# Strassen products for 16 of 22 row tiles of the FFN down projection, set between the gate/up tiles

## The reference

```python
D_FF = -(-8 * D_MODEL // (3 * 256)) * 256          # 2816
def _swiglu(x, w_gu, w_down):
    gate, up = jnp.split(x @ w_gu, 2, axis=-1)
    return (jax.nn.silu(gate) * up) @ w_down
...
        h = _layernorm(ALPHA * h + mix, ln_mix_g[i], ln_mix_b[i])
        h = _layernorm(ALPHA * h + _swiglu(h, ffn_w_gu[i], ffn_w_down[i]), ln_ffn_g[i], ln_ffn_b[i])
```

## Time and profile before

| | |
|---|---|
| median of three executions | 2300.27 us |
| the profiled execution | 2299.87 us |
| its span, first to last instruction | 2298.1 us |
| mean granted clock of TensorE | 0.996 of full |
| busy share PE / DVE / ACT / POOL | 98% / 31% / 31% / 45% |
| read from HBM | 211.02 MB, 93 GB/s over the span |

### The profile page before, as it was taken

One profiled execution on the slowest core, in us unless ns is written; L12 is line 12 of the kernel. 1 busy time (PEld: TensorE's weight loads), 2 busy tenths in 40 slices (PEclk: granted clock), 3 DMA queues, 4 the chain that ended last, 5 costly groups with the idle time before them and its releaser, 6 DMA issues.

```text
span 2298.1 us, 24743 instructions
## 1 busy us (share of the span) xinstructions
PE 2259.6 (98%) x10303; PEld 1826.6 (79%) x10303; DVE 702.9 (31%) x1405; ACT 708.3 (31%) x1009; POOL 1025.3 (45%) x350
## 2 busy tenths in 40 slices
PE   8999999999999999999999999999999999999998
PEld 6667888888777778888888888888887667888887
DVE  7535000003467450010048420000159625000004
ACT  2453221221344332213222232222235572221220
POOL 3224554554332345545445655445433334554453
PEclk9999999999999999999999999999999999999999
DMA  4122323222212232222222332322212213222221
GB/s 173 60 89 98 122 93 109 92 74 92 92 69 79 74 110 92 94 108 83 101 93 98 108 110 96 106 92 83 101 64 102 77 43 147 92 92 94 105 77 55
DMA packets 33535, 214.72 MB, mean 93 GB/s; under 512 B 3720, under 2 KB 4872, under 8 KB 10000
## 3 DMA queue, kind: packets, MB, share of 16 engines
q1 hardware_dynamic: 32256, 211.03, 26.2%
q10 hardware_dynamic: 1168, 2.11, 0.3%
HBM read 211.02 MB, written 2.11 MB: 93 GB/s over the span
## 4 chain that ended last, share of the span: by engine, by line
PE 89%; DVE 8%; ACT 2%; issue 1%; POOL 1%; DMA 0%; SPq 0%; DVEq 0%; ACTq 0%
PE bank L1005 17%; PE bank L1007 16%; PE bank L1006 16%; PE bank L1055 9%; PE bank L1057 9%; PE bank L1056 9%; DVE bank L2138 3%; PE bank L1200 2%; PE bank L1195 2%; PE bank L1196 2%; PE bank L1499 1%; PE bank L1240 1%; PE bank L1473 1%; PE bank L1094 1%; PE bank L1116 1%
## 5 line engine op out<-in xcount | busy, mean ns | idle before, releaser
L848 POOL TENSOR_TENSOR wlo<-raw,whi 128x2048 fp32r<-128x2048 f32 (+5 forms) x184 | 843.3, 4586 | 657.0 <-ACT whi L479 647.0
L1005 PE MATMUL bank<-XH,whi 128*128 128x512 f32 x1720 | 678.7, 395 | 6.2 <-POOL wlo L904 6.2
L1007 PE MATMUL bank<-XH,wlo 128*128 128x512 f32 x1720 | 671.2, 390 | 0.0
L1006 PE MATMUL bank<-XL,whi 128*128 128x512 f32 x1720 | 670.9, 390 | 0.0
L479 ACT CAST whi<-raw 128x2048 fp32r<-128x2048 f32 (+5 forms) x184 | 349.4, 1901 | 378.1 <-PE bank L1055 304.3
L1005 PEld LDWEIGHTS bank<-XH,whi 128*128 128x128 f32 x1720 | 323.8, 188 | 86.2 <-issue 14.0
L1007 PEld LDWEIGHTS bank<-XH,wlo 128*128 128x128 f32 x1720 | 323.7, 188 | 68.4
L1006 PEld LDWEIGHTS bank<-XL,whi 128*128 128x128 f32 x1720 | 324.0, 188 | 65.0
L1811 DVE TENSOR_TENSOR hf<-sil,bank 128x512 f32<-128x512 f32 x80 | 55.0, 688 | 814.4 <-PE bank L1007 814.4
L1055 PE MATMUL bank<-whi,HH 128*128 128x512 f32 x704 | 274.4, 390 | 0.0
L1057 PE MATMUL bank<-wlo,HH 128*128 128x512 f32 x704 | 274.0, 389 | 0.0
(11 more groups left out here) (280 smaller groups left out, 2172.2 us busy)
## 6 DMA issues: line engine op xcount, KB each, us to landing
raw<-w_ffn_gu SPq DMA_DIRECT2D x88, 1024.0 KB, 4.9
raw<-w_ffn_dn SPq DMA_DIRECT2D x40, 1024.0 KB, 4.8
GB<-gb SPq DMA_DIRECT2D x8, 1024.0 KB, 6.9
raw<-w_diff_in SPq DMA_DIRECT2D x6, 1280.0 KB, 6.5
raw<-w_ev_in SPq DMA_DIRECT2D x6, 1024.0 KB, 5.0
raw<-w_od_in SPq DMA_DIRECT2D x4, 1536.0 KB, 6.5
raw<-w_mla_pair SPq DMA_DIRECT2D x4, 1088.0 KB, 5.5
raw<-w_mla_o SPq DMA_DIRECT2D x4, 1024.0 KB, 5.9
```

What stands on the lines that cost most here:

```text
L848: pool.tensor_tensor(wlo[:, off:off + size], raw[:, off:off + size], whi[:, off:off + size].bitcast(F32), ALU.subtract).then_inc(lo_ready, 1)
L1005: release(pe.matmul(out, whi[:, off:off + P], xh, start=start, stop=False))
L1006: pe.matmul(out, whi[:, off:off + P], xl, start=False, stop=False)
L1007: return pe.matmul(out, wlo[:, off:off + P], xh, start=False, stop=stop)
```

## The change

The first 16 row tiles of the down weight form two chunks of 8 (`CHUNK`). For a chunk the product of hidden values (512 tokens x 1024) and weight (1024 x 1024) is cut in 2 x 2 blocks on each side, and the eight block products are replaced by Strassen's seven. Each is a sum of two blocks of the left side, or one block, times a sum of two blocks of the weight, or one. `PRODUCTS` lists them: the left blocks and their sign, the weight block that the unit loads, the sign with which the weight block of the unit before is combined, and the quarters of the output that the result goes into. A product is 2 token blocks x 4 row tiles x 3 passes = 24 matmuls of 512 columns. The last 6 row tiles (`REST`) stay with the old scheme, in groups of 2 and 4 (`DOWN`).

The order of the units is `FFN_ORDER`: gate/up 0 to 8, then products 0 to 6 in turn with gate/up 9 to 15, then gate/up 16 to 20 in turn with products 7 to 11, gate/up 21, products 12 and 13. The four down units follow. An FFN has 40 units in place of 34.

A product's unit goes another way through the engines. DVE sums `raw` of the unit and of the product unit before it into `BS` (`block_sum`), ACT casts `BS` (or `raw`) to `whi` (`split_block`), DVE subtracts to `wlo` (`low_block`). For the left side DVE sums blocks of the hidden values, which now stay in float32 in `HF`, into `AS` (`left_sum`), ACT casts to `AH`, POOL subtracts to `AL` (`split_left`). DVE adds a result from PSUM into one or two quarters of `X` (`add_product`).

```diff
-HID = (12, 10)
+CHUNK = 8
+HIDDEN = D_FF // P
+REST = HIDDEN - 2 * CHUNK
...
-DOWN = ((4, 4, 4), (2, 4, 4))
+DOWN = (2, 4)
+
+FFN_ORDER = [("gu", j) for j in range(CHUNK + 1)]
+for _i in range(7):
+    FFN_ORDER += [("st", _i), ("gu", CHUNK + 1 + _i)]
+for _i in range(5):
+    FFN_ORDER += [("gu", 2 * CHUNK + _i), ("st", 7 + _i)]
+FFN_ORDER += [("gu", HIDDEN - 1), ("st", 12), ("st", 13)]
...
+PRODUCTS = (((0, 0), (0, 1), 1, (1, 1), 0, ((0, 0, -1), (0, 1, 1))),
+            ((0, 0), None, 0, (0, 1), -1, ((0, 1, 1), (1, 1, 1))),
+            ((1, 0), (0, 0), -1, (0, 0), 1, ((1, 1, 1),)),
+            ((1, 0), (1, 1), 1, (0, 0), 0, ((1, 0, 1), (1, 1, -1))),
+            ((1, 1), None, 0, (1, 0), -1, ((0, 0, 1), (1, 0, 1))),
+            ((0, 1), (1, 1), -1, (1, 1), 1, ((0, 0, 1),)),
+            ((0, 0), (1, 1), 1, (0, 0), 1, ((0, 0, 1), (1, 1, 1))))
...
SP, load:
-                sp.wait_ge(lo_ready, max(overlaps, u - SEMS) + 1)
+                plain, sums = raw_free(u)
+                sp.wait_ge(lo_ready, plain)
+                if sums:
+                    sp.wait_ge(bsum_ready, sums)
...
ACT, ffn:
+                for n in range(2, FFN_UNITS - 1):
+                    if n + 2 < DOWN_AT and FFN_ORDER[n + 2][0] == "st":
+                        q = 14 * ffns.n + FFN_ORDER[n + 2][1]
+                        split_block(q)
+                        if q % 7:
+                            split_left(q)
+                    elif n + 2 < FFN_UNITS or not last:
                         split_w()
+                    if n + 1 < DOWN_AT and FFN_ORDER[n + 1][0] == "st" and FFN_ORDER[n + 1][1] % 7 == 0:
+                        split_left(14 * ffns.n + FFN_ORDER[n + 1][1])
...
POOL:
+            def split_left(q):
+                pool.wait_ge(asum_hi, q + 1)
+                pool.tensor_tensor(AL[q % 2][:], left(q), AH[q % 2][:].bitcast(F32), ALU.subtract).then_inc(asum_lo, 1)
...
PE:
+            def strassen(q):
+                off, i = begin_unit(), q % 2
+                pe.wait_ge(asum_lo, q + 1)
+                for r in range(2):
+                    b, rows = 4 + 2 * i + r, slice(r * P, (r + 1) * P)
+                    claim(b)
+                    for k in range(4):
+                        cols = slice(off + k * HALF, off + (k + 1) * HALF)
+                        release(pe.matmul(bank[b][:], AH[i][:, k, rows], whi[:, cols], start=k == 0, stop=False))
+                        pe.matmul(bank[b][:], AL[i][:, k, rows], whi[:, cols], start=False, stop=False)
+                        ins = pe.matmul(bank[b][:], AH[i][:, k, rows], wlo[:, cols], start=False, stop=k == 3)
+                    ins.then_inc(acc_done, 1)
...
DVE:
+            def block_sum(q):
...
+                dve.wait_ge(raw_ready[u % SEMS], 16 * (u // SEMS + (1 if u % SEMS else 0)))
+                dve.wait_ge(bsum_lo, q)
+                dve.tensor_tensor(BS[:], raw[:, own:own + 2048], raw[:, prev:prev + 2048],
+                                  ALU.add if PRODUCTS[q % 7][4] > 0 else ALU.subtract).then_inc(bsum_ready, 1)
...
+                for n in range(2, DOWN_AT + 1):
+                    if block_at(n + 2) is not None:
+                        low_block(block_at(n + 2))
+                        if block_at(n + 2) % 7:
+                            left_sum(block_at(n + 2))
+                    if block_at(n + 1) is not None and block_at(n + 1) % 7 == 0:
+                        left_sum(block_at(n + 1))
+                    if block_at(n - 1) is not None:
+                        add_product(block_at(n - 1))
+                    if block_at(n + 3) is not None:
+                        block_sum(block_at(n + 3))
+                    if n < DOWN_AT and FFN_ORDER[n][0] == "gu":
+                        j = FFN_ORDER[n][1]
+                        dst = HF[j // CHUNK][:, j % CHUNK, :] if j < 2 * CHUNK else sil[j % 2][:]
                         dve.wait_ge(gate_done, gates.at(1))
-                        take(lambda: dve.tensor_tensor(hf[i][:], sil[i][:], bank[2 * i + 1][:], ALU.mult), 2)
+                        take(lambda: dve.tensor_tensor(dst, sil[j % 2][:], bank[2 * (j % 2) + 1][:], ALU.mult), 2)
```

More of the change, by code:

```diff
@@ L116, with unit_kinds, sums_to, left_sums_to @@
 UNITS = unit_table()
+def unit_kinds():
+    plain, ffns, kinds = 0, 0, []
+    for u, (name, i, size, off, over) in enumerate(UNITS):
+        if name.endswith("_st"):
+            first = next(v for v in range(u, -1, -1) if not UNITS[v][0].startswith(name[:4]))
+            q = 14 * int(name[3]) + FFN_ORDER[u - first - 1][1]
+            kinds.append((None, q))
+        else:
+            plain += 1
+            kinds.append((plain, None))
+    return kinds
+KINDS = unit_kinds()
+BLOCK_UNIT = {q: u for u, (plain, q) in enumerate(KINDS) if q is not None}
+def sums_to(q):
+    return len(SUMS) * (q // 7) + sum(1 for i in SUMS if i <= q % 7)
+def left_sums_to(q):
+    return len(LEFT_SUMS) * (q // 7) + sum(1 for i in LEFT_SUMS if i <= q % 7)
+def raw_free(u):
+    name, i, size, off, over = UNITS[u]
+    plain, sums = 0, 0
+    for v in range(u):
+        o, n = UNITS[v][3], UNITS[v][2]
+        if v != u - SEMS and (o >= off + size or off >= o + n):
+            continue
+        if KINDS[v][0] is not None:
+            plain = max(plain, KINDS[v][0])
+        else:
+            q = KINDS[v][1]
+            sums = max(sums, sums_to(q + 1 if q % 7 + 1 in SUMS else q))
+    return plain, sums
 SEMS = 4
@@ L480, in split_w, with split_block @@
                     unit.add()
+            def split_block(q):
+                name, i, size, off, overlaps = UNITS[unit.n]
+                assert KINDS[unit.n][1] == q
+                act.wait_ge(w_used, overlaps + 1)
+                if q % 7 in SUMS:
+                    act.wait_ge(bsum_ready, sums_to(q))
+                    act.copy(whi[:, off:off + size], BS[:]).then_inc(bsum_hi, 1)
+                else:
+                    act.wait_ge(raw_ready[unit.n % SEMS], 16 * (unit.n // SEMS + (1 if unit.n % SEMS else 0)))
+                    act.copy(whi[:, off:off + size], raw[:, off:off + size]).then_inc(bsum_hi, 1)
+                unit.add()
             def split_x(dst, src):
@@ L832, in _ @@
                     tiles.add(3)
+            lows.add(4)
             odd_high(3)
@@ L978, in begin_unit @@
             def begin_unit(retire=1):
-                pe.wait_ge(lo_ready, unit.at(1))
+                plain, q = KINDS[unit.n]
+                if plain is not None:
+                    pe.wait_ge(lo_ready, plain)
+                else:
+                    pe.wait_ge(bsum_lo, q + 1)
                 off = UNITS[unit.n][3]
@@ new lines, in low_block, with left_sum @@
+            def low_block(q):
+                off = UNITS[BLOCK_UNIT[q]][3]
+                dve.wait_ge(bsum_hi, q + 1)
+                src = BS[:] if q % 7 in SUMS else raw[:, off:off + 2048]
+                dve.tensor_tensor(wlo[:, off:off + 2048], src, whi[:, off:off + 2048].bitcast(F32), ALU.subtract).then_inc(bsum_lo, 1)
+            def left_sum(q):
+                first, second, sign = PRODUCTS[q % 7][0:3]
+                c = q // 7 % 2
+                if sign:
+                    if q:
+                        dve.wait_ge(asum_lo, 7 * ((q - 1) // 7) + max(i for i in LEFT_SUMS if i <= (q - 1) % 7) + 1)
+                    dve.wait_ge(tile_free, tiles.at())
+                    dve.wait_ge(eh_ready, earlies.at())
+                    dve.tensor_tensor(AS[:], corner(c, *first), corner(c, *second),
+                                      ALU.add if sign > 0 else ALU.subtract).then_inc(asum_ready, 1)
@@ new lines, in add_product @@
+            def add_product(q):
+                seen = {}
+                for i in range(q % 7):
+                    for th, d, sign in PRODUCTS[i][5]:
+                        seen[th, d] = True
+                dve.wait_ge(acc_free, accs.at())
+                for r in range(2):
+                    b = 4 + 2 * (q % 2) + r
+                    dve.wait_ge(acc_done, accs.at(1))
+                    for th, d, sign in PRODUCTS[q % 7][5]:
+                        x, op = xhalf(2 * th + r, d), ALU.add if sign > 0 else ALU.subtract
+                        if q // 7 % 2 == 0 and (th, d) not in seen:
+                            ins = dve.scalar_tensor_tensor(x, x, ALPHA, bank[b][:], ALU.mult, op)
+                        else:
+                            ins = dve.tensor_tensor(x, x, bank[b][:], op)
+                    ins.then_inc(acc_free, 1)
+                    accs.add()
```

160 lines of the change are left out of this document (96 added, 64 removed).

## The result

The changed kernel takes **2264.67 us** (median of four executions, 2262.41 to 2265.91), against 2299.93 of the kernel before in the same session (2298.01 to 2301.23). The ratio is 0.9846, with a 95% interval of 0.9829 to 0.9863, so 35.3 us or 1.5% less. The prediction said 2266, in a range from 2257 to 2282. The profiled execution took 2262.41 us, its span is 2260.6 us.

A forecast was written before the change was run, and what follows sets the result against it. PE, nearly always busy, was taken as the bound: matmuls times spacing plus waits. 2299.87 - 43.5 + 7.8 + 1.3 = 2265.5; with the median 0.4 above that execution, 2266 us, range 2257 to 2282.

The forecast's parts named there:

- The matmuls, -43.5: On PE: two chunks and four FFNs make 192 matmuls fewer, at 0.2267 us each 43.5 us off.
- The body of the FFN, 0: Work added off PE in each FFN stays hidden behind PE's matmuls, product 13 with 3.0 us spare: 0 us.
- The chain at its tightest: Chunk 2, period 16.32 us of one product and one gate/up unit: AL done at 10.5, needed at 16.3.
- Who goes first at the port: Where DVE's two-SBUF-input operations and POOL exclude each other: a waiting DVE goes first between two POOL instructions.
- The norm, 7.8 + 1.3: Layer norm behind each FFN: PE waits for DVE, 2.6 us in each of the first three, 1.3 behind the last.
- near 8: Sign of being right: PE's waits for X at the transposes near 8 us in all.
- the collision: Norm's block 0: DVE's two-input step waits for POOL's low half, and its pair of steps loses about 0.9 us.
- (a): Rival at the norm: it costs nothing more, port free and DVE keeping pace; 2257 us; chance 0.08.
- (b): Rival at the port: POOL goes first when both wait, weight sums end 4.6 later; 2270 to 2282 us; chance 0.20.
- (c): Rival: slower than before, as the port also serves DVE's additions and gate multiplications; 72 us, 2338; chance 0.09.
- (d): Rival at the products: an unseen cost per product, say 0.4 us x 56, eats half the gain; 2288; chance 0.07.
- throughout: PE's granted clock: the top step in all 40 slices, read as 2.4 GHz throughout.

## Why the prediction was right, step by step

- **The matmuls, -43.5: right.** 192 fewer, and by the two kernels with more and fewer of them 0.22 to 0.23 us each. The period of a product and a gate/up tile is 16.32 us to the hundredth. The 131 ns that the Trainium skill (TensorE: Matmul & The Clock Gate, Back-to-back issue gap) gives would have made them worth 25 us by estimate, and no run here agrees.
- **The body of the FFN, 0: right, and for the reasons given.** The chain at its tightest was worked out with AL at 10.5 us of the period. In one period it is at 10.5, in the one with the most work at 12.6, since there a weight sum came ahead of it; 16.3 is the limit. The low half of the gate/up unit was put at 17.4 and is at 17.15. The durations estimated from a line through two widths hold: 2.29 and 1.22, measured 2.30 and 1.22. Product 13 had 3.5 us spare where the sum said 3.0, and the kernel with AL twice found that limit.
- **Who goes first at the port: the rule held, the timetable did not.** The assumption was that a waiting DVE gets in between two POOL instructions. Where it was already waiting, it did (the three rows of the last section). But the sum had AL until 10.5 us in every period, with the weight sum waiting behind it, and no term for the four additions ahead of the weight sum. In two periods of each FFN the product takes a single block of hidden values, there is no left sum, and AL was over at 8.06. The additions kept DVE until 8.09. The weight sum was then 0.07 us behind the start of POOL's low half, whose whole 4.61 it waited, to 14.8 us and not 12.8. The next gate multiplication was due at 16.6, so 1.8 us of DVE's time made the result safe.
- **The norm, 7.8 + 1.3: the mechanism right, the size 1.0 too large.** Measured 7.1 + 1.0 = 8.1. In the first FFN the transposes of block 2 would by the same working start 17.9 us behind its zero and start at 19.95, so 2.1 are lost up to there and not 2.6. Another 0.3, for which the sum had no term, goes since these eight transposes are drawn out behind a wait. The row of the waits itself shows 5.2 us, where "near 8" was to be the sign. The terms: the collision 0.77 for 0.9, DVE's pace 5.60 for 5.70, and the last FFN 1.0 for 1.3, by DVE's 4.41 us a block in place of 4.5.
- **The rivals.** (a) falls: the norm costs 8.1 us. (b), POOL going first when both wait, was not seen; the delay it described stands in two periods of each FFN, by another cause, and is free. (c) falls: additions and gate multiplications take 0.69 us whatever POOL does. (d) falls: no idle time ahead of a product, and the body's periods have no seam.
- **The clock: "throughout" was too much.** It fell to the lower level for moments in both kernels, at places outside the FFNs and their norms, and no term of the sum stands for that.

For the profiled execution the sum gave 2265.5, and it took 2262.41. Of the 3.1 us between them 1.0 are the norm's. The other 2.1 (1.3 + 1.6 - 0.8) are scatter of the two executions, most of it the clock's. The medians differ by 1.3: 0.9 of it is the size of the loss, and the median of the kernel before came out 0.3 lower with a fourth execution.

## What to carry to other kernels

Where the matrix engine is always busy, a saving of matmuls is worth their spacing, measured over whole units, less what the other engines can no longer hide, and that is to be sought at the place where their work has become shortest on PE's side, not where most has been added. A chain with 3.5 us spare takes new work for nothing up to that and charges all beyond it, and a stop of 2.7 us was charged again by the clock, with 1.7. Long GpSimd instructions should start when VectorE has turned to operands in PSUM; shorter pieces at the wrong moment are worse than one long one at a harmless one.

## What the runs showed of the hardware

- **The port is held by whole instructions.** 0.07 us made the difference between a weight sum of 2.29 us and one of 6.69. It works in both directions: at 490.69 POOL's AL took 3.57 in place of 2.40, behind DVE's low half of 489.69. And where DVE's weight sum began 0.05 us ahead of AL, at 477.91, the sum took its 2.29 and AL 4.50. The Trainium skill (Trainium Architecture — The Big Picture, What this means for kernel authors) calls this port pair an exclusive lock and no split of bandwidth. The trace agrees.
- **A waiting DVE gets in between two GpSimd instructions.** In the kernel with half of the matmuls, POOL, DVE, POOL:

```profile
454.87 2.40 POOL L1011 TENSOR_TENSOR AL<-AS,AH 128x1024 fp32r<-128x1024 f32 x1 [4.56 <-ACT AH L622]
...
455.17 4.26 DVE L1974 TENSOR_TENSOR BS<-raw 128x2048 f32<-128x2048 f32 x1 [0.27 <-DMA raw<-w_ffn_st]
...
457.23 6.66 POOL L974 TENSOR_TENSOR wlo<-raw,whi 128x2048 fp32r<-128x2048 f32 x1
```

DVE's sum (2.29 us alone) waits for POOL's AL until 457.2 and ends at 459.4, and POOL's next, good for 4.61, ends 2.05 late.
- **The lower clock after short stops.** After 2.7 us without a matmul the granted clock was 0.50, at all four places of the kernel with half of the matmuls (1.7 us lost behind each). The same happened in the kernel with the pieces ahead of DVE's steps after the first of its stops of 2.02 us, hidden there behind DVE:

```profile
560.00:562.00 2.00, 2.00 (x7) 0.50 0.00 0
```

But not every such stop does it. In that same trace the third of these norms has stops of 2.02 and 1.85 us and keeps 1.00. All eleven traces share a stop of 2.1 us (in the kernel before at 786.6), and the clock fell after it in four of them. They share one of 1.65 to 1.8 us, and it fell in five. It fell in all eleven after a stop of 2.4 us (in the kernel before at 1867.8), in three after two stops of 1.0 and 0.7 us close to each other, and in none after the four single stops of 1.3 us in the kernel with AL twice. So up to 2.1 us the same stop of nearly the same program was followed by either level. It shows in the time: the changed kernel took 2262.41 us with a mean granted clock of 0.998, and 2265.41 and 2265.91 with 0.995.
